# A hybrid decoder layer in fp32: pairs of projection sections by seven block products

## The reference

```python
PROJ_SIZES = (HG_KDIM, HG_KDIM, HG_WIDTH, HG_WIDTH,
              DA_WIDTH, DA_WIDTH, DA_WIDTH, DA_WIDTH, D_MODEL, D_MODEL)

u = rmsnorm(h, norm_g[l])
proj = jnp.einsum('bld,de->ble', u, w_in[l])
hq, hf, hi, hz, aq, ak, av, az, ga, gb = jnp.split(proj, offs, axis=-1)
f = lb + (1.0 - lb) * jax.nn.sigmoid(hf.astype(jnp.float32))
kA = 1.0 - f
oA = hgrn2_chunked(q, log f, kA, hi)                   # S_t = diag(f_t) S_{t-1} + k_t^T v_t
oA = merge_heads(rmsnorm(oA.astype(dt), hg_norm_g[l]))
yA = jnp.einsum('blw,wd->bld', oA * jax.nn.silu(hz), w_branch_a[l])
oB = diff_attention(q1, k1, q2, k2, vh, lam)           # causal, rotary on a quarter of the dims
oB = merge_heads(rmsnorm(oB, da_norm_g[l]) * (1.0 - lam_init))
yB = jnp.einsum('blw,wd->bld', oB * jax.nn.silu(az), w_branch_b[l])
m = jax.nn.sigmoid(ga) * yA + jax.nn.sigmoid(gb) * yB
h = h + jnp.einsum('bld,de->ble', m, w_out[l])
out = rmsnorm(h, final_g)
```

## Time and profile before

| | us |
|---|---|
| median of 3 runs | 753.9 |
| lowest, highest | 752.92, 754.2 |
| the profiled execution | 753.44 |
| its span in the trace | 751.7 |
| of it ahead of head 0's first level | 48.1 |
| seven heads, each | 62.9 |
| last head and merge up to w_out's end | 253 |

### The profile page before, as it was taken

The page is one execution under the profiler, slowest core; times in us unless marked ns, Lnnn a source line. Parts: engine busy times, 40 slices in busy tenths (PEclk is TensorE's granted clock), DMA queues, the critical chain, the costliest instruction groups (busy, mean ns, idle before and its releaser), DMA issues.

```text
span 751.7 us, 12966 instructions
## 1 busy us (share of the span) xinstructions
PE 731.2 (97%) x4665; PEld 653.9 (87%) x4665; DVE 453.1 (60%) x1019; ACT 281.0 (37%) x548; POOL 23.0 (3%) x34
## 2 busy tenths in 40 slices
PE   2999999999999999999999999999999999999996
PEld 2998999999899899999989989998888888888885
DVE  4567569568667856956866785695643333233342
ACT  5414442642552444264155235425423222232232
POOL 2000000000000000000000000000000000000000
PEclk9899999999999999999999999999999999999999
DMA  7421220230122132023012213302323323323603
GB/s 265 122 76 57 86 84 12 72 112 28 56 87 81 50 90 84 2 82 112 28 56 84 84 35 104 85 1 85 112 85 112 95 87 98 112 84 98 237 29 113
DMA packets 105416, 63.44 MB, mean 84 GB/s; under 512 B 2066, under 2 KB 100772, under 8 KB 105396
## 3 DMA queue, kind: packets, MB, share of 16 engines
q1 hardware_dynamic: 105076, 62.52, 27.5%
q10 hardware_dynamic: 320, 0.66, 0.3%
HBM read 61.07 MB, written 2.10 MB: 84 GB/s over the span
## 4 chain that ended last, share of the span: by engine, by line
PE 96%; SPq 1%; issue 1%; DMA 1%; DVE 0%; ACT 0%; POOLq 0%; POOL 0%; DVEq 0%; ACTq 0%
PE ps L385 26%; PE ps L386 26%; PE ps L387 26%; PE ps L506 3%; PE ps L576 2%; PE ps L602 2%; PE ps L492 1%; PE ps L593 1%; PE ps L603 1%; PE ps L540 1%; PE ps L539 1%; PE ps L547 1%; PE ps L522 1%; DMA rows_in<-in_da_norm_g 1%; PE ps L531 1%
## 5 line engine op out<-in xcount | busy, mean ns | idle before, releaser
L385 PE MATMUL ps<-uT_hi,w_hi 128*128 128x512 f32 (+3 forms) x960 | 321.6, 335 | 0.0
L386 PE MATMUL ps<-uT_lo,w_hi 128*128 128x512 f32 (+3 forms) x960 | 308.7, 322 | 0.0
L387 PE MATMUL ps<-uT_hi,w_lo 128*128 128x512 f32 (+3 forms) x960 | 307.9, 321 | 0.0
L385 PEld LDWEIGHTS ps<-uT_hi,w_hi 128*128 128x128 f32 x960 | 181.6, 189 | 16.4 <-issue 3.2
L252 DVE TENSOR_TENSOR w_lo<-w_raw,w_hi 128x1024 fp32r<-128x1024 f32 x104 | 127.1, 1222 | 109.9 <-ACT w_hi L247 108.9
L387 PEld LDWEIGHTS ps<-uT_hi,w_lo 128*128 128x128 f32 x960 | 181.1, 189 | 13.9
L386 PEld LDWEIGHTS ps<-uT_lo,w_hi 128*128 128x128 f32 x960 | 181.6, 189 | 11.6
L247 ACT ACTIVATE w_hi<-w_raw 128x1024 fp32r<-128x1024 f32 x104 | 109.4, 1052 | 87.5 <-PE ps L387 84.3
L808 ACT ACTIVATE e<-e,small 128x144 f32<-128x144 f32 (+3 forms) x64 | 36.1, 565 | 41.9 <-DVE small L1200 41.9
L375 POOL TENSOR_TENSOR small<-small 128x4 f32<-128x4 f32 x16 | 16.1, 1008 | 507.3 <-DVE small L1135 362.7
L1133 DVE TENSOR_REDUCE small<-sq 128x4 f32<-128x512 f32 x16 | 11.0, 686 | 33.3 <-ACT sq L800 33.3
(11 more groups left out here) (185 smaller groups left out, 993.4 us busy)
## 6 DMA issues: line engine op xcount, KB each, us to landing
w_raw<-in_w_in SPq DMA_DIRECT2D x80, 512.0 KB, 3.7
w_raw<-in_w_branch_a SPq DMA_DIRECT2D x8, 512.0 KB, 3.6
w_raw<-in_w_branch_b SPq DMA_DIRECT2D x8, 512.0 KB, 3.6
w_raw<-in_w_out SPq DMA_DIRECT2D x8, 512.0 KB, 3.8
x_in<-in_x SPq DMA_DIRECT2D x4, 512.0 KB, 7.8
x_res<-in_x SPq DMA_DIRECT2D x4, 512.0 KB, 6.4
out<-y_out SPq DMA_DIRECT2D x8, 256.0 KB, 2.3
rope<-in_c_rope SPq DMA_DIRECT2D x1, 528.0 KB, 6.0
```

Of the source, the lines that this page charges most:

```text
L385: pe.matmul(dst, w[0], rhs[0], start=start, stop=False, skip_group_check=True)
L386: pe.matmul(dst, w[0], rhs[1], start=False, stop=False, skip_group_check=True)
L387: return pe.matmul(dst, w[1], rhs[0], start=False, stop=stop, skip_group_check=True)
```

## The change

**Pairs.** HF with HQ, AK with AQ, and ga with gb of the same d are made as one product: left the weights, as 2 by 2 blocks (rows: first and second 128 output channels, columns: first and second 512 input channels), right the input, as 2 by 2 blocks (512 channels and 256 tokens each). Seven block products take the place of eight (`PARTS = 7`, function `part`). Four of them need sums of weight blocks, made for each pair; four need sums T1 to T4 of input blocks, made once in head 0 (`t_hi`, `t_lo`). Their order is P1, P5, P7, P2, P3, P6, P4: j = 0 and 3 accumulate in bank 0 on plain blocks, the meta tokens with them except in gates; j = 6 uses a plain input block; j = 1, 2, 4, 5 use T.

**Weight sums.** `w_sum` gets HQ's (AQ's, gb's) first block once more from HBM and the second is added to it by a DMA that accumulates (`add_s1`); s3 is an accumulating DMA in the raw buffer (`add_s3`). `sum_2` and `sum_4` run on DVE.

**Low parts.** Of three units of a head (HZ, AV, AZ) and of parts 3 and 4 of a pair ACT also writes the negated high part into `w_lo` and an accumulating DMA adds the raw weights. The other five parts and HI (in two halves) stay with DVE. All eleven accumulating DMAs of a head are issued by POOL, as are its two powers.

**Combinations.** ACT saves P1 and P5; DVE makes five sums and differences of 256 columns per pair (`comb_75`, `comb_16`, `comb_21`, `comb_22`, `comb_12`), which give the outputs.

**Order.** A head pass has 60 steps: HI, HZ, AV, AZ (32), then 2 x 14 half parts. A slot is now half a unit (8 slots). The tables of steps are moved one or two steps ahead. The gates of d = 2 to 7 are made in a row after the heads with two sets of raw buffers, then 16 branch units in a new order. oa and ob are split into high and low parts after the heads, in fours. Head 0 is written out ahead of ACT's and DVE's loops. The second step of the rotary on keys stands after level 1 on DVE. The weights are laid out in HBM so that a unit's partition is one row of 4 KB (8 pieces of 512 bytes before).

```diff
-SLOTS = 4
+BLK = 512
+SLOTS = 8
...
+HI_ORDER = (0, 3, 1, 2, 4, 5, 6)
+BY_VECTOR = (0, 1, 2, 5, 6)
...
-HG_AT = dict(zip(HG_STEPS, (3, 8, 11, 14, 17, 20, 23, 26, 30, 33, 36, 41)))
-AT_AT = dict(zip(AT_STEPS, (23, 23, 30, 33, 33, 36, 38, 41, 43, 45, 47, 52, 54, 60)))
+HG_AT = dict(zip(HG_STEPS, (2, 7, 10, 13, 16, 19, 22, 25, 30, 33, 36, 42)))
+AT_AT = dict(zip(AT_STEPS, (21, 21, 30, 33, 33, 36, 37, 40, 42, 44, 46, 51, 53, 59)))
...
+    def part_hi(act, q, j, r, loads, i, free):
+
+        if j in (5, 6):
+            act.wait_ge(sums, 2 * q + j - 4)
+        elif j == 1:
+            act.wait_ge(s1_added, 16 * q + 16)
+        elif j == 2:
+            act.wait_ge(s3_added, 16 * q + 16)
+        else:
+            act.wait_ge(w_loaded[r + 1 if j == 4 else r], 16 * loads)
+        act.wait_ge(w_used, free)
+        act.activation(blk(w_hi, i), part_src(r, j), ACT.Copy).then_inc(pair_hi, 1)
+        if j not in BY_VECTOR:
+            act.activation(blk(w_lo, i), part_src(r, j), ACT.Copy, scale=-1.0).then_inc(part_neg, 1)
+
+    def part_lo(dve, q, j, r, i):
+
+        dve.wait_ge(pair_hi, PARTS * q + HI_ORDER.index(j) + 1)
+        dve.tensor_tensor(blk(w_lo, i), part_src(r, j), blk(w_hi, i).bitcast(F32), ALU.subtract).then_inc(pair_lo, 1)
+
+    def sum_2(dve, q, r):
+
+        dve.wait_ge(s1_added, 16 * q + 16)
+        dve.wait_ge(s3_added, 16 * q + 16)
+        dve.wait_ge(pair_lo, LOWS * q + 1)
+        a_11 = raw_at(r)[:, 0:BLK]
+        dve.tensor_tensor(a_11, sum_at(r), a_11, ALU.add).then_inc(sums, 1)
...
+            def units_of_head(h):
+
+                sp.wait_ge(lo_ready, UNITS + h + 1)
+                sp.sem_inc(slot_free, 1)
+                columns(h, AV, 0)
+                sp.wait_ge(unit_added[0], 16 * h + 16)
+                sp.sem_inc(slot_free, 1)
+                columns(h, AZ, 1)
+
+            def pair_of_head(h, r, h_next, cols):
+
+                q = 2 * h + r
+                if r == 0:
+                    sp.wait_ge(unit_added[1], 16 * h + 16)
                     sp.sem_inc(slot_free, 1)
...
+                else:
+                    sp.wait_ge(pair_lo, LOWS * q)
+                    sp.sem_inc(slot_free, 1)
+                columns(h_next, cols[0], 0)
+                base_21(h_next, cols[1], 0)
+                if r == 0:
+                    sp.wait_ge(unit_added[2], 16 * h + 16)
+                else:
+                    sp.wait_ge(part_added[1], 16 * q)
+                sp.sem_inc(slot_free, 1)
+                columns(h_next, cols[1], 1)
...
+            def add_unit(h, n, r, slot):
+
+                pool.wait_ge(unit_neg, 3 * h + n + 1)
+                pool.sem_inc(adds_begun, 1)
+                pool.dma_start(w_lo[:, slot, :], raw_at(r), accum_op=ALU.add).then_inc(unit_added[n], 16)
+
+            def add_s3(q, r, loads):
+
+                pool.wait_ge(w_loaded[r], 16 * loads)
+                pool.wait_ge(w_loaded[r + 1], 16 * loads)
+                pool.sem_inc(adds_begun, 1)
+                pool.dma_start(raw_at(r + 1)[:, 0:BLK], raw_at(r)[:, 0:BLK], accum_op=ALU.add).then_inc(s3_added, 16)
...
+            def part(q, j, half, i, lo_done, meta):
+
+                from_ = 0 if meta else META
+                if half == 0:
+                    pe.wait_ge(*lo_done)
+                    if j == 3:
+                        pe.wait_ge(p1_saved, q + 1)
+                    elif j == 4:
+                        pe.wait_ge(comb, 10 + 5 * q + 1)
+                    elif j == 5:
+                        pe.wait_ge(c11_taken, q + 3)
+                for k in (2 * half, 2 * half + 1):
+                    if j in (0, 3):
+                        dst = bank(0)[:, from_:META + HALF]
+                        rhs = tuple(a[:, (0 if j == 0 else KT // 2) + k, from_:META + HALF] for a in (uT_hi, uT_lo))
+                    elif j == 6:
+                        dst = bank(2)[:, 0:HALF]
+                        rhs = tuple(a[:, KT // 2 + k, META + HALF:TOK] for a in (uT_hi, uT_lo))
+                    else:
+                        dst = bank({1: 2, 2: 1, 4: 1, 5: 0}[j])[:, 0:HALF]
+                        rhs = tuple(a[:, {1: 0, 2: 2, 4: 3, 5: 1}[j], k, :] for a in (t_hi, t_lo))
+                    w = tuple(blk(a, i)[:, k * P:(k + 1) * P] for a in (w_hi, w_lo))
+                    last = three(dst, w, rhs, j in (0, 1, 2, 5) and k == 0, k == KT // 2 - 1)
+                if half == 1:
+                    last.then_inc(w_used, 1)
```

982 lines of the change are left out of this document (674 added, 308 removed).

## The result

The changed kernel takes **768.25 us** (median of 4 runs, 765.8 to 771.57) against 753.7 us for the kernel before (752.92 to 754.2): a ratio of 1.0197, 95% interval 1.0148 to 1.0245. It is 14.5 us slower where 738 had been predicted; the range reached to 758. The interval lies wholly above 1 and on both sides of 1.02, so the kernel is slower, but whether by more than 2% stays open.

What follows compares the result with a forecast made beforehand. The prediction took PE, busy 97% of the span, as the bound. Its terms were 753.4 - 28.3 + 5 (head 0) + 4.9 (small waits) + 2.2 (handover) = 737.2, given as 738 us, range 728 to 758.

Steps and rivals of the forecast that it cites:

- What PE loses: PE's products in heads and gates: seven in place of eight save 2.72 us a head, 28.3 us in all.
- The other engines: Per head, DVE goes from 44.7 to 47.5 us and ACT from 25.8 to some 32.4; neither bounds by its sum.
- Head 0: In the first head DVE also makes the T matrices, so PE waits: +5 us, bounds 2 and 8.
- The price of an accumulating DMA: POOL's eleven adds a head: 5.0 us for 512 KB and 3.7 for 256 KB, issue included.
- The test that the prediction named: Landing time of POOL's 512 KB DMAs: 5 us or less carries the forecast, over 6 breaks it.
- The longest chain: In a normal head, HZ, AZ, HQ, s3, then ACT's copies: slack just used up, PE waits 0 to 0.4 us.
- Rival D: In every head, the HZ-AZ-HQ-s3 chain outgrows covered time (adds 7.0 and 5.0 us): about 773 us; chance 0.16.
- The tight places: Turns, halves of HI and out_21 in seven heads: slacks of 0.2 to 1.7 us, 0.7 us a head, +4.9.
- Handover and gate phase: From last head to gates: PE waits 1.7 us for a low part, 0.5 for s1 and s3; +2.2 (0 to 5).
- After that nothing: Gate phase behind the handover: PE needs 9.95 us a pair, DVE 7.0, ACT some 7.5, raw buffers cover loads; no loss.
- The tail: The program's end was claimed to stay as before, with no added time.
- C: Rival: adds somewhat longer (5.7 and 4.2 us), or DVE's and ACT's orders collide at the turns: 748 us; chance 0.20.

Runs made afterwards that it cites:

- experiment 1: The changed kernel with all accumulating DMAs left out, POOL only raising the semaphore in their place: 739.57 us, ratio 0.9819.
- experiment 6: The changed kernel with ACT taking vT_b, the first exponentials and k_tok ahead of the high parts that wait for s1 and s3: 762.44 us, ratio 1.0118.
- experiment 4: The changed kernel with the gate phase's two low parts per pair made by DVE in place of accumulating DMAs, heads unchanged: 762.73 us, ratio 1.0121.

## Why the prediction was wrong, point by point

**What PE loses: right.** The products that read the T matrices start 16 steps in 209.05 to 210.96, 119.4 ns each (118.5 taken). Without adds a head takes 60.9 us, and 60.2 + 0.7 was forecast: of the gain of 2.7 us a head at least 2.0 is there. The prediction's price of a slower start in these products counts all 84 matmuls of a pair, where only 48 read T: 1.1 us per ns and not 1.8. It wasn't needed.

**The other engines: right** to 0.2 us (DVE) and 1 us (ACT) a head. As was said there, the sums did not decide.

**Head 0: right in kind, small in size.** 66.8 us against 65.2; without adds 65.8, so 1 of the 1.6 us goes with the adds.

**The price of an accumulating DMA: right, and it misled.** 4.5 us for 512 KB undisturbed where 5.0 was taken, 3.3 for 256 KB where 3.7 was. The formula of the Trainium skill (DMA: Bandwidth & Descriptors, section on the anatomy of one DMA on the GpSimd path), 3.2 and 2.6 us, was cited beside it; the trace disagrees, with 4.5 and 3.3 for these DMAs, which also read their destination. The test that the prediction named, a landing time of 5 or 6 us, was put on the wrong number.

**The longest chain: this step failed.** It was found and written down in the right order, and its end came 2.7 us late. 0.6 of that is HZ's start and hand-over to SP, 2.1 are one term: **the load of AZ, priced at 3.9 us with its issue, took 6.0**, because it is issued when HZ's add lands, in the same few us in which AV's add (6.0 us there; AZ's, of the same size, takes 4.5) is under way. Without any add the same load took 3.3 us (experiment 1). In heads 3 and 4 the load of AZ took 4.3 and 4.2 us, and AZ's add, 4.5 in the others, took 7.3 and 7.0 beside the two loads behind it; these heads are the longest, 64.1 and 63.9 us. ACT won 0.5 back and HQ's load 0.4, s3 lost 0.7: its 4.3 us stand behind the 0.55 of s1's issue and 0.5 from SP's load to POOL's first DMA. Every transfer had been taken as if it were alone, and the DMA share of 0.23 that spoke for that the earlier trace rows was the one of the kernel before; after, it is 0.55. The change itself filled the DMA engines. Rival D had this chain, but looked for the growth in the length of an add. The growth of 2.7 us that it named as the point where the whole gain is eaten is the one measured, and that is chance: by D's own subtraction of the half us left, 2.7 costs 8 x 2.2 = 17.6 us, less than the 21.1 (28.3 - 7.2) that it needs, and the point lies at 3.1. That its 773 lies near 768 is luck too, since about half of what is over the forecast comes from behind the heads.

**Then ACT's queue made 2.4 us a head of it.** The same late s3 costs PE a wait at vT_b or k_tok and another at the values; by the traces of experiment 6, 1.4 us of it is the order in which ACT was told to wait; by the medians it is 0.8.

**The tight places: the size came out by luck.** Without adds a head takes the 60.9 us that base and allowance made, but PE is busy for 60.88 of 60.90 us in head 2: there are no waits there. Nor does PE wait at a turn in heads 1 to 6 of the changed kernel. The 0.7 us stood for waits and covered matmuls that start a little later than priced, such as the 119.4 ns above for 118.5; which ones make it up wasn't separated.

**Handover and gate phase: this step failed too, and by more** (17.1 us with the last head). The handover was put at 2.2 us, 1.7 for the first block's low part and 0.5 for s1's. They took 1.81 and 2.98, and then the clock cost 1.4, which no term had; even without adds it is a wait of 1.8 us and a stretch at half clock. "After that nothing" was worked out from the sums of ACT's and DVE's times and from two sets of raw buffers, that is from throughput. But a pair's low part by DMA stands in front of sum_4 and of the loads that follow, and 83% busy DMA engines made up to 8.0 us of its 3.3. The phase took 75.2 us, with these low parts on DVE 70.5 (experiment 4), and without any add it takes 64.9. A chain had been walked for the heads and none for the gates.

**The tail: 2.8 us that no step had.** It is told under the last heading.

**The chances.** The side "slower" had 0.16, all of it rival D, and the cases between C and D were given as sizes of the adds, beside orders that collide at the turns. If crowding had been asked for by name, the chain's slack of 0.5 us would have been seen to be less than any doubt on its seven terms.

## What to carry to other kernels

When a step moves from an engine with slack to a DMA, ask first what waits for the transfer to release its source: the buffer is held until it lands. Reading the addend from HBM in place of the buffer made each transfer of 512 KB 3 us slower (those of 256 KB 0.6), and the kernel 14.7 us faster. Price transfers by the DMA share that the change will cause, not by the one of the profile before, and walk the longest chain in every phase, also where all the sums fit. Two engines that wait in order pass a delay on: put what waits for a transfer behind what doesn't.
